# Differential attention: the combined map is turned by VectorE in 32x32 blocks and moved into place by SBUF transfers instead of being transposed on TensorE

## What is computed

```python
def diff_attention(h, w_qkv, w_o, lam, subln, cos, sin, layer_idx):
    B, S, _ = h.shape                                  # 1, 512
    H, d = DIFF_HEADS, DIFF_HEAD_DIM                   # 8 heads, d = 64
    q, k, v = jnp.split(h @ w_qkv, 3, axis=-1)
    q = apply_rope(q.reshape(B, S, 2 * H, d), cos, sin)
    k = apply_rope(k.reshape(B, S, 2 * H, d), cos, sin)
    v = v.reshape(B, S, H, 2 * d)
    ...
    def one_block(qb):
        s = jnp.einsum('bqhd,bkhd->bhqk', qb, k).astype(jnp.float32) * scale
        pr = jax.nn.softmax(s, axis=-1).reshape(B, H, 2, DIFF_Q_BLOCK, S)
        a = (pr[:, :, 0] - lam_full * pr[:, :, 1]).astype(v.dtype)
        return jnp.einsum('bhqk,bkhe->bqhe', a, v)
    ...
    o = rms_norm(o, subln) * (1.0 - lam_init)
    return o.reshape(B, S, H * 2 * d) @ w_o
```

## Time and profile before

| | us |
|---|---|
| median of three runs | 1958.52 |
| lowest and highest | 1957.97, 1958.56 |
| profiled execution, its own time | 1956.75 |
| its span, from first to last instruction | 1954.9 |
| TensorE busy in the span | 1930.3 (99%) |
| VectorE, ScalarE, GpSimd busy | 1176.4, 923.8, 1107.9 |
| granted TensorE clock, mean | 0.997 |

### The profile page before, as it was taken

One profiled execution on the slowest core, in us unless ns is written; L12 is line 12 of the kernel. 1 busy time (PEld: TensorE's weight loads), 2 busy tenths in 40 slices (PEclk: granted clock), 3 DMA queues, 4 the chain that ended last, 5 costly groups with the idle time before them and its releaser, 6 DMA issues.

```text
span 1954.9 us, 25157 instructions
## 1 busy us (share of the span) xinstructions
PE 1930.3 (99%) x9200; PEld 1589.6 (81%) x9200; DVE 1176.4 (60%) x1978; ACT 923.8 (47%) x1752; POOL 1107.9 (57%) x848
## 2 busy tenths in 40 slices
PE   8999999999999999999999999999999999999998
PEld 6878888888888887777888888888787888888887
DVE  6773325353433488776774746756688775746755
ACT  5644336533333366554543443445577543433443
POOL 5335544454444457554675666664874576656653
PEclk9999999999999999999999999999999999999999
DMA  4122233233232332112323322323211323222321
GB/s 170 57 71 97 95 110 129 95 105 103 97 111 97 101 105 76 54 55 70 128 94 108 98 86 97 108 87 108 72 44 33 130 98 103 98 91 97 99 95 65
DMA packets 53705, 182.71 MB, mean 93 GB/s; under 512 B 5840, under 2 KB 8272, under 8 KB 53584
## 3 DMA queue, kind: packets, MB, share of 16 engines
q1 hardware_dynamic: 53584, 181.12, 28.0%
HBM read 174.80 MB, written 6.29 MB: 93 GB/s over the span
## 4 chain that ended last, share of the span: by engine, by line
PE 96%; DVE 3%; ACT 0%; issue 0%; DMA 0%; SPq 0%; DVEq 0%; ACTq 0%
PE b L397 29%; PE b L405 29%; PE b L401 29%; PE b L427 3%; PE b L417 1%; PE b L454 1%; PE b L465 1%; PE b L449 1%; PE b L420 1%; PE b L421 1%; PE b L475 0%; PE b L434 0%; PE b L440 0%; PE b L441 0%; DVE ra L639 0%
## 5 line engine op out<-in xcount | busy, mean ns | idle before, releaser
L241 POOL TENSOR_TENSOR ra<-raw,ra 128x512 fp32r<-128x512 f32 x632 | 876.5, 1395 | 756.9 <-ACT ra L285 755.3
L397 PE MATMUL b<-ra 128*128 128x512 f32 (+1 forms) x2560 | 890.2, 392 | 11.0 <-ACT ra L285 7.5
L405 PE MATMUL b<-ra 128*128 128x512 f32 (+1 forms) x2560 | 877.0, 387 | 0.0
L401 PE MATMUL b<-ra 128*128 128x512 f32 (+1 forms) x2560 | 876.7, 387 | 0.0
L285 ACT ACTIVATE ra<-raw 128x512 fp32r<-128x512 f32 x632 | 392.0, 628 | 521.9 <-PE b L405 513.4
L397 PEld LDWEIGHTS b<-ra 128*128 128x128 f32 x2560 | 480.9, 188 | 109.8 <-issue 10.6
L405 PEld LDWEIGHTS b<-ra 128*128 128x128 f32 x2560 | 481.0, 188 | 98.9
L401 PEld LDWEIGHTS b<-ra 128*128 128x128 f32 x2560 | 482.0, 188 | 94.0 <-DVE ra L500 0.4
L755 DVE TENSOR_TENSOR h<-b,h 128x512 f32<-128x512 f32 x136 | 91.5, 682 | 56.1 <-PE b L405 55.5
L646 DVE TENSOR_TENSOR tmp<-b,rb 128x512 f32<-128x512 f32 x66 | 45.2, 690 | 109.4 <-PE b L405 109.1
L639 DVE TENSOR_TENSOR ra<-b,ra 128x512 fp32r<-128x512 f32 (+4 forms) x166 | 92.1, 566 | 22.3 <-ACT ra L336 20.3
(11 more groups left out here) (277 smaller groups left out, 1806.7 us busy)
## 6 DMA issues: line engine op xcount, KB each, us to landing
raw<-in_f_g SPq DMA_DIRECT2D x40, 512.0 KB, 3.4
raw<-in_f_v SPq DMA_DIRECT2D x40, 512.0 KB, 3.5
raw<-in_f_d SPq DMA_DIRECT2D x40, 512.0 KB, 3.4
raw<-in_w_up SPq DMA_DIRECT2D x32, 512.0 KB, 3.5
raw<-in_w_down SPq DMA_DIRECT2D x32, 512.0 KB, 3.4
raw<-in_p_g SPq DMA_DIRECT2D x16, 512.0 KB, 3.4
raw<-in_w_gp SPq DMA_DIRECT2D x8, 512.0 KB, 3.5
raw<-in_w_ga SPq DMA_DIRECT2D x8, 512.0 KB, 3.5
```

The costliest lines, as they stand in the source:

```text
L241: e.tensor_tensor(wl, src, wh.bitcast(F), ALU.subtract).then_inc(*w_low.mark(n))
L397: e.matmul(m.banks[b][:, 0:xh.shape[-1]], wh[:, c:c + 128], xh, start=start, stop=False)
L401: e.matmul(m.banks[b][:, 0:xh.shape[-1]], wh[:, c:c + 128], xl, start=False, stop=False)
L405: last = e.matmul(m.banks[b][:, 0:xh.shape[-1]], wl[:, c:c + 128], xh, start=False, stop=stop)
```

## The change

Only `attention_diff` uses the new path; the other attentions keep `heads`.

- The combined map of query tile i still lands in `fa`, of which now four buffers hold maps. VectorE then transposes each 32x32 block of it in place of its block (`flip`, one instruction of 512 columns per tile), into `Z`, the other four buffers of `fa`. Blocks are transposed, but they are not yet on the right partitions.
- After four flips SP issues 16 transfers within SBUF (`move`), each 32 partitions by 2 KB (64 KB), 1 MB for a head, from `Z` into the low half of the map's `ra` slots. They wait for the last flip and for the product of the head before. All 16 are issued on the queue that also carries the weights.
- The moved float32 map is split in two halves of 1024 columns: ScalarE rounds each (`round`), then VectorE subtracts for the first and GpSimd for the second (`rest`), in place.
- `pv_moved` is again 12 matmuls of 512 columns; the moving operand is read in runs of 32 columns.
- The 128 TensorE transposes of maps, the 32 `turn_high` and the 32 `turn_low` of this layer are gone. The first flip of a head waits for the moves of the head before.
- The planner gets durations: 9.0 us for a move, 0.62 for a flip, 2.74 for the product, 1.1, 1.25 and 2.7 us for the parts on ScalarE, VectorE and GpSimd.

```diff
+        elif kind == "move":
+            dst, src, before, moved = a
+            for t in before:
+                w.wait_ge(*t)
+            for i in range(4):
+                for j in range(4):
+                    e.dma_start(dst[32 * j:32 * j + 32, S * i:S * i + S],
+                                src[32 * i:32 * i + 32, S * j:S * j + S]).then_inc(*moved.mark(n, 16))
...
+        elif kind == "pv_moved":
+            (vh, vl), pt, b, high, ready = a
+            dst = m.banks[b][:, :].rearrange("p (i j a) -> p i j a", i=4, j=4)
...
+            for kt in range(4):
+                e.matmul(dst, vh[:, 128 * kt:128 * kt + 128], pt[0][:, kt], start=kt == 0, stop=False)
...
+        elif kind == "flip":
+            z, p, made, free = a
+            w.wait_ge(*made)
+            for t in free:
+                w.wait_ge(*t)
+            e.transpose(z, p).then_inc(*soft.mark(n))
...
+        if kind == "pv_moved":
+            return 2.74
...
+    if engine == "sp":
+        return 9.0
+    if kind in ("round", "rest") and a[0].shape[-1] == 2 * S:
+        return dict(ac=1.1, ve=1.25, gp=2.7)[engine]
...
+    if kind == "flip":
+        return 0.62
...
+    def heads_moved(n, VT, O, PTb, P_of, p_done, rank):
+
+
+        raised = [m.ra[:, PTb + 2 * z:PTb + 2 * z + 2, :, :].rearrange("p a b c -> p (a b c)") for z in range(2)]
+        pt = [x.rearrange("p (j i k a) -> p k i j a", i=4, j=4, k=4) for x in raised]
+        Z = fa[:, 4:8, :].rearrange("p a b -> p (a b)")
+        at = Z.rearrange("p (j i k a) -> p i k j a", i=4, j=4, k=4)
+        flipped, moved, low, used = {}, {}, {}, {}
+
+        def flips_of(t):
+            for i in range(4):
+                yield 0, "ve", lambda: None if (t, i) not in p_done or (t and t - 1 not in moved) else (
+                    p_done[(t, i)], *([moved[t - 1]] if t else []))
+                x = done("ve", "soft_v", row("flip", at[:, i], P_of(t, i).rearrange("p (k j a) -> p k j a", j=4, a=32),
+                                             p_done[(t, i)], (moved[t - 1],) if t else ()))
+                P_of(t, i, x)
+                flipped[(t, i)] = x
+            if t + 1 < n:
+                launch(flips_of(t + 1))
+
+        def move_of(t):
+            yield 0, "sp", lambda: None if (t, 3) not in flipped or (t and t - 1 not in used) else (
+                flipped[(t, 3)], *([used[t - 1]] if t else []))
+            before = (flipped[(t, 3)], *([used[t - 1]] if t else []))
+            moved[t] = done("sp", "moved", row("move", raised[1].bitcast(F), Z, before, m.sig("moved")))
+            for half, eng in enumerate("vp"):
+                def tell(y, half=half):
+                    low[(t, half)] = y
+                sl = slice(1024 * half, 1024 * half + 1024)
+                launch(parts_of((raised[0][:, sl], raised[1][:, sl]), raised[1][:, sl].bitcast(F), (moved[t],), eng,
+                                lambda: (used[t - 1],) if t else (), tell))
+            if t + 1 < n:
+                launch(move_of(t + 1))
...
-        PB = Pool([fa[:, i, :] for i in range(8)])
+        PB = Pool([fa[:, i, :] for i in range(4)])
...
-        heads(n, VT, span, O, PTb, P_of, p_done, lambda t: 8 * t + 8, 2, wide_tbk, n - 1, wide_sbk)
+        heads_moved(n, VT, O, PTb, P_of, p_done, lambda t: 8 * t + 16)
```

More of the change, by code:

```diff
@@ L443, in tensor_program @@
             x.then_inc(*pv.mark(n))
+        elif kind == "pv_moved":
+            (vh, vl), pt, b, high, ready = a
+            dst = m.banks[b][:, :].rearrange("p (i j a) -> p i j a", i=4, j=4)
+            for t in high:
+                w.wait_ge(*t)
+            for kt in range(4):
+                e.matmul(dst, vh[:, 128 * kt:128 * kt + 128], pt[0][:, kt], start=kt == 0, stop=False)
+            for t in ready:
+                w.wait_ge(*t)
+            for kt in range(4):
+                e.matmul(dst, vl[:, 128 * kt:128 * kt + 128], pt[0][:, kt], start=False, stop=False)
+                x = e.matmul(dst, vh[:, 128 * kt:128 * kt + 128], pt[1][:, kt], start=False, stop=kt == 3)
+            x.then_inc(*pv.mark(n))
         elif kind == "pv_halves":
@@ L853, in __init__ @@
         self.last = {}
-        self.clock = dict(pe=0.0, ve=0.0, ac=0.0, gp=0.0)
+        self.clock = dict(pe=0.0, ve=0.0, ac=0.0, gp=0.0, sp=0.0)
         self.begun, self.ended = [], {}
@@ L1368, in heads, with products_of, need @@
         launch(products_of(0))
+    def heads_moved(n, VT, O, PTb, P_of, p_done, rank):
[27 more added lines that the diff above has]
+                launch(move_of(t + 1))
+        def products_of(t):
+            def need():
+                if VT(t) is None or (t, 0) not in low or (t, 1) not in low or bank_free[obk] is None:
+                    return None
+                return (*VT(t)[-1], low[(t, 0)], low[(t, 1)], *bank_free[obk])
+            yield rank(t), "pe", need
+            *values, vt = VT(t)
+            lows, free = (low[(t, 0)], low[(t, 1)]), tuple(bank_free[obk])
+            x = row("pv_moved", values, pt, obk, (*vt, *high_of(lows), *free), (*vt, *lows, *free))
+            bank_free[obk] = None
+            used[t] = done("pe", "pv", x)
+            heads_used.add(t)
+            launch(O(t, used[t]))
+            if t + 1 < n:
+                launch(products_of(t + 1))
+        launch(flips_of(0))
+        launch(move_of(0))
+        launch(products_of(0))
```

## The result

| | before | after |
|---|---|---|
| median of four runs beside each other, us | 1958.24 | 1971.73 |
| lowest and highest | 1957.91, 1958.56 | 1969.47, 1973.35 |
| profiled execution, its own time | 1956.75 | 1973.35 |
| its span | 1954.9 | 1971.2 |

The change makes the kernel slower: after takes 1.0068 of before's time, 95% interval 1.0056 to 1.008. The forecast was 1949.4. Nearly all of the difference lies in the stage: in the profiled executions its last residual addition starts at 950.65 us before and at 966.66 after, 16.0 us later, and the whole span is 16.3 longer. (The profiled execution of after is the slowest of its four; between the medians it is 13.5.)

What follows compares the result with a forecast made beforehand. TensorE, busy in 99% of the span, was taken as the bound. 1956.75 - 14.1 (turns) + 3 (stage end) + 2 (heads) = 1947.7; on the median, 1958.52 - 9.1 = 1949.4 us, range 1943.5 to 1954, chance 0.62.

Steps and rivals of the forecast that it cites:

- The move: 16 transfers within SBUF per head: 8.2 us at 0.37 us per issue, ends 7.1 and 14.1, against 9.0 planned.
- The rival of the slow move: TensorE waits ahead of each head's first low product, 8 x (move - 9.1); 1987 us at 14.1; chance 0.16.
- In the steady state the new chain is no bound: Between heads: 13.7 us from last map to product fits a head's period of about 24 us.
- The queues: Weight loads behind the 16 issues on SP: costed at nothing, since SP sat idle 207.5 us.
- The end of the stage: Head 7's longer chain into part d makes TensorE wait: 3 us, range 0 to 6.
- A planner takes spread and sums at once: At the stage's end, with nothing else left, planner margin between square and column sums goes; with all gone, no wait.
- The turns: 32 turns (128 transposes) leave TensorE at 0.44 us each: 14.1 us gained, all on the path setting the end.
- The strided operand: Product's moving operand in runs of 32 columns: costed at nothing; rival at half speed 22 us, 1971, chance 0.05.
- the flips: VectorE's 32 block transposes of 512 columns: 0.74 us each, 23.7 us.
- the subtraction: VectorE's subtraction of 1024 columns: 1.22 us each, 8 of them 9.8 us.
- the roundings: ScalarE's 16 roundings of 1024 columns: at most 19.1 us, equal to the 19.1 lost, so no change.
- VectorE and GpSimd in each other's way: Rival: one wait per head for a whole 2.6 us GpSimd instruction, 12 us more, 1961, no change; chance 0.10.

Runs made afterwards that it cites:

- e1_plan127: The changed kernel with the planner told 12.7 us for a move instead of 9.0: 1968.08 us, 1.0049 of before.
- e6_last_on_pe: The changed kernel with 12.7 us planned for a move and head 7's maps turned by TensorE as before: 1958.09 us, 1.0001 of before.
- e8_loads_later: e6_last_on_pe with a weight load put into SP's order only when its slot is due to be empty: 1953.38 us, 0.998 of before.
- e2_wide4: The changed kernel with a move of 4 issues of 128 partitions by 2 KB, change of partitions left out: 1948.51 us, 0.9952 of before.
- e11_before_loads_later: The kernel before with only the later entry of weight loads from e8_loads_later: 1958.43 us, 1.0002 of before.
- e4_turn1: The kernel before with one of four transposes in each turn of this layer, 96 left out: 1948.68 us, 0.9953 of before.
- e9_by_hbm: e8_loads_later with the move by way of HBM, one 1 MB store then 4 loads, 10.0 us planned: 1961.19 us, 1.0017 of before.
- e12_both_on_vector: e8_loads_later with both large subtractions on VectorE, none on GpSimd: 1955.25 us, 0.999 of before.

## Why the prediction was wrong

The kernel without any wait would be at 1958.2 - 14.1 = 1944.1. After lies 27.6 above that. The runs divide it so:

| part | us | from |
|---|---|---|
| plan of 9.0 for a move of 11.9 | 3.7 | after - e1_plan127 |
| head 7's longer chain at the end | 11.8 | e1_plan127 - e6_last_on_pe, + 1.8 |
| moves behind a waiting load | 4.7 | e6_last_on_pe - e8_loads_later |
| not separated | 7.4 | the rest |

The parts hold the idle time and the clock lost with it, since each run gives both. The rest has the stretched subtractions, the waits that e8_loads_later still has (3.5 us, 2.4 more than before), and lost clock. The least certain part is the first: the intervals of after (1.0056 to 1.008) and e1_plan127 (1.0034 to 1.0064) overlap. The order of the edits matters for such a division: it was made once, in this one. It divides by places; by cause most of it is one thing, the length of the move, since e2_wide4 with its 6 us has 23.2 of the 27.6 us back at one stroke.

Step by step:

- **The move** failed, in its size. I took 0.37 us per issue from stores to HBM; an issue within SBUF takes 0.59. The move takes 11.9 us and not 8.2: inside my ends of 7.1 and 14.1, and beyond the 10.2 at which I put the sign to turn and the 10.8 from which I called it slower. The row nearest in bytes was the wrong one to go by, and the back-to-back rows that gave the upper end were nearer. My choice inside the range, and a chance of 0.16 for the other case, were the error. e2_wide4 shows what hung on it: with a move of some 6 us the same kernel comes to 1948.5.
- **The rival of the slow move** is what happened. Its law, 8 x (move - 9.1), gives 22 us for 11.9, so 1969.8; measured are 1971.7, and after is 23.2 above e2_wide4. The total fits better than its working. The law puts all of it ahead of the products, eight times. There TensorE waits only 9.0 us, for five of the eight heads (2.30, 0.68 and 1.48, 0.88, 2.57, 1.06); the rest came ahead of scores, at the end of the stage and by the clock. That the two agree so well is in part luck.
- **"In the steady state the new chain is no bound"** was wrong. VectorE waited for a move before its flips seven times, 23.1 us. I took the mean period of a head and looked at the last ones, where 16 us lie between a head's last scores (872) and the next head's first (888). In the early heads of before it is 9, 11 and 8 us (738 to 747, 756 to 767, 775 to 783), less than a move.
- **The queues**: wrong in what I looked at. I priced loads behind a move at nothing, and no run shows a cost there; e11_before_loads_later shows only that later loads cost nothing without moves. The price was on the other side, moves behind a load that waits: 4.7 us. (The 207.5 us of SP's idle time are those of 720 to 930; to 940 they are 216.4 in 26 waits, which changes nothing.)
- **The end of the stage** is where most of it fell due: 3 us (0 to 6) against 11.8. Of my own working, the longer move accounts for 3.7 and the rest is what follows in order, column sums, spread and the last splits, each waited for anew in e1_plan127 (3.35, 1.44, 1.86 and 1.50), and a clock of 0.83 behind them. With the short move of e2_wide4 the waits there are 0.35 and 1.50, so the 3 us would have done. "A planner takes spread and sums at once" did not come: each has a chain on VectorE and ScalarE of its own.
- **The clock** had no term. Every wait was priced at its own length, and in after they cost up to half as much again: 17.8 us idle, at most 8.5 of lost clock. In the trace -14.1 for the turns, 16.7 more idle time and 8.5 of clock give 11.1 of the 16.0 us; 4.9 are in neither. About 1.0 of them is the product, see below; for the others there is no row.
- **The turns**: 14.1 us stands, as e4_turn1 and the distances in its trace show.
- **The strided operand** costs little: the product's matmuls start 0.238 us apart at full clock, on average, where before's start 0.228 apart. That is 1.0 us over 96, not the 22 of the rival, whose 1971 us meet the measured time by chance.
- **Right**: the flips at 0.70 us (0.74 forecast), the subtraction's 1.2 us where nothing is in its way (1.22 forecast), GpSimd's 2.5 (2.6), the roundings. VectorE and GpSimd in each other's way were a rival with 12 us more: the runs show the clash, its price in e8_loads_later is at most the 7.4 us not separated, and in after it has a part in the wait of 2.30 us too.

That the sum without the slow move was right, 1949.4 beside 1948.5 in e2_wide4, is half luck. The forecast had 5 us against the gain of the turns, as waits at the end and in the heads. In e2_wide4 about 4.7 stand against it, and they are other things: 1.8 us more idle time, up to 1.75 of lost clock and about 1.0 in the product. Its move is also shorter than the 8.2 us of the forecast, and a kernel with that move was not run.

## What to carry to other kernels

A chain of many small transfers costs the issue time of each on its queue; measure that for the very pair of memories before planning on it, and count issues before bytes. When work leaves the bounding engine for a longer chain, ask for the last item of the stage first, because nothing hides it there: keeping the old way for the last head, with the plan mended, turned the change from slower to no difference. And in an in-order queue look at what a latency-critical transfer stands behind, not only at what it holds up.

## What the runs showed of the hardware

- A DMA issue on SP with both ends in SBUF took 0.59 to 0.60 us in the median at 64 and 256 KB, in 32 and in 128 partitions; SBUF to HBM took 0.33 to 0.38 (e9_by_hbm), HBM to SBUF 0.33 to 0.44 there and 0.46 or 0.72 each for four in a row in before. The first load behind a move mostly took 0.58.
- A 32x32 block transpose of 128x512 float32 on VectorE took 0.67 to 0.71 us, about as much as a plain subtraction of that size, 0.683.
- A transposition of 128x128 on TensorE costs 0.11 us within a stream, though the row lists 0.27; by the time of e4_turn1, which holds some added waits, it is 0.096.
- A moving operand in runs of 32 columns (128 bytes) cost 0.238 us for 512 columns at full clock, beside 0.228 for one run of 512: 4% more.
- After TensorE's waits of 1.91 us and more in after, its granted clock fell to 0.50 (1.2 GHz) for some 3 to 7 us; after those of 1.50 and less it stayed. It is no fixed rule: it fell behind a wait of 1.50 us in e2_wide4, e6_last_on_pe and e12_both_on_vector, e8_loads_later has windows of 5 us at 0.75 and 0.57 behind a wait of 0.91 us, and e9_by_hbm a wait of 2.30 us with one matmul of 0.50 us and then 0.40 us each behind it, full clock. What decides is open.
